# The convolution's norm, from a stage of its own into the branch stage

## What is computed

```python
y = conv(up) + conv_b                          # depthwise, 31 taps
y = jax.nn.silu(layernorm(y, ln_g, ln_b))      # mean and variance over the 1024 channels
y_c = (y * jax.nn.silu(g_conv)) @ w_conv_out   # the convolution's branch
o = sparse_attention(q, k, v, qi, ki, wi, past, rel_bias)
y_a = (o * jax.nn.silu(g_attn)) @ w_attn_out   # attention's branch
y = (gm_c * y_c + gm_a * y_a) @ w_out          # gates gm_c, gm_a per channel
```

## Time and profile before

| | us |
|---|---|
| three runs | 3887.52, 3889.7, 3890.3 (median 3889.7) |
| profiled execution, its own time | 3887.92 |
| its span | 3886.2 |
| norm stage, first issue to attention's first | 142.96 |
| branch stage, first issue to output's first | 400.00 |
| PE busy over the span | 3498.8 (90%) |
| DVE, ACT, POOL busy | 2761.4 (71%), 1359.0 (35%), 1145.0 (29%) |

### The profile page before, as it was taken

How to read it: one execution, slowest core, us unless ns; L and a number is a source line. 1 busy time by engine, 2 the same in 40 slices (tenths; PEclk the granted TensorE clock), 3 DMA queues, 4 the chain that set the end, 5 groups by cost and what they waited for, 6 DMA issues and landing times. The chain is left out here.

```text
span 3886.2 us, 50171 instructions
## 1 busy us (share of the span) xinstructions
PE 3498.8 (90%) x18975; PEld 2933.9 (75%) x18975; DVE 2761.4 (71%) x4366; ACT 1359.0 (35%) x1623; POOL 1145.0 (29%) x1004
## 2 busy tenths in 40 slices
PE   5869888999998999999753999989989998999998
PEld 1868777999998999999621555555556555999987
DVE  1431667999998699999755788787787776554434
ACT  2211556776710000100043555555545555000121
POOL 2233001543343000000003464464463332444300
PEclk9989999999999999999885999999999999999999
DMA  7274426445557344444444211211211111575643
GB/s 275 70 234 157 120 88 157 154 161 180 190 174 259 126 148 158 154 164 167 152 158 113 61 32 32 63 31 31 65 28 31 30 31 64 190 239 172 207 137 116
DMA packets 389362, 497.40 MB, mean 128 GB/s; under 512 B 52152, under 2 KB 298056, under 8 KB 388683
## 3 DMA queue, kind: packets, MB, share of 16 engines
q10 hardware_dynamic: 124144, 246.15, 18.9%
q1 hardware_dynamic: 252939, 203.55, 18.0%
q0 software_dynamic: 12112, 45.65, 3.2%
HBM read 305.62 MB, written 195.67 MB: 129 GB/s over the span
## 5 line engine op out<-in xcount | busy, mean ns | idle before, releaser
L991 PE MATMUL psum<-ha,gt 128*128 128x352 f32 x8352 | 1373.6, 325 | 46.7 <-POOL gt L629 28.6
L991 PEld LDWEIGHTS psum<-ha,gt 128*128 128x128 f32 x8352 | 1362.8, 189 | 51.2 <-POOL gt L629 28.9
L1243 DVE SCALAR_TENSOR_TENSOR cv<-cv,vecs,cv 128x1056 f32<-128x1056 f32 (+1 forms) x480 | 598.9, 1326 | 0.0
L1997 DVE TENSOR_TENSOR at_plo<-at,at 128x1024 fp32r<-128x1024 f32 (+2 forms) x308 | 402.1, 1307 | 134.8 <-ACT at L1893 133.9
L1892 ACT ACTIVATE at<-psum 128x1024 f32<-128x1024 f32 (+2 forms) x308 | 293.1, 952 | 495.2 <-PE psum L1774 495.1
L1819 PE MATMUL psum<-at,at 128*128 128x512 f32 (+5 forms) x688 | 337.9, 497 | 137.7 <-DVE at L1927 53.4
L642 PE MATMUL psum<-br,br 128*128 128x352 f32 x2304 | 375.7, 324 | 16.1 <-POOL br L620 15.5
L642 PEld LDWEIGHTS psum<-br,br 128*128 128x128 f32 x2304 | 374.0, 189 | 17.1 <-POOL br L620 13.6
L716 DVE TENSOR_SCALAR_CACHE_REDUCE gl<-gt,gl 128x1792 bf16<-128x1792 f32 (+5 forms) x325 | 383.2, 1246 | 1.2
L627 POOL TENSOR_TENSOR gt<-gt,ones 128x1024 fp32r<-128x1024 f32 x64 | 133.3, 2082 | 646.7 <-PE psum L991 522.0
L687 ACT ACTIVATE gl<-gt,gl 128x2048 bf16<-128x2048 f32 (+9 forms) x160 | 265.6, 1661 | 92.4 <-DVE gl L732 77.6
(11 more groups left out here) (239 smaller groups left out, 4783.3 us busy)
## 6 DMA issues: line engine op xcount, KB each, us to landing
scratch_ws<-gt ACTq DMA_DIRECT2D x112, 512.0 KB, 6.1
gt<-scratch_ws ACTq DMA_DIRECT2D x112, 512.0 KB, 5.0
gt<-in_w_in_dram ACTq DMA_DIRECT2D x64, 512.0 KB, 5.3
scratch_gm<-gt ACTq DMA_DIRECT2D x32, 528.0 KB, 3.1
br<-scratch_gm ACTq DMA_DIRECT2D x32, 528.0 KB, 3.6
scratch_m<-br POOLq DMA_DIRECT2D x32, 528.0 KB, 4.1
at<-scratch_q SPq DMA_DIRECT2D x128, 128.0 KB, 2.8
su<-in_ada_w_dram SPq DMA_DIRECT2D x6, 2048.0 KB, 22.3
```

Of the source, the lines that this page charges most:

```text
L991: ins = nc.tensor.matmul(of[:, j, 0:W // 3], wt[b][:, c, :], a[:, c, j * (W // 3):(j + 1) * (W // 3)], start=(c == 0 and k == 0), stop=(c ...
L1243: ins = nc.vector.scalar_tensor_tensor(to[:, 0:width], mine[:, k_:k_ + width], tap, to[:, 0:width], ALU.mult, ALU.add)
L1997: nc.vector.tensor_tensor(plo[j % 3][:, 0:len(mine), 0:n], prob[j % 3][:, 0:len(mine), 0:n], phi[j % 3][:, 0:len(mine), 0:n].bitcast(F32), ...
```

## The change

`norm_stage` and its scratch array c are gone. `branch_stage` runs (half 0, a), (half 1, a), (half 0, c), (half 1, c), all written out without loops. Beside the 8 blocks of a run with attention of half 1 (run 1) it norms the convolution's half 0, and beside run 2 half 1, in three chunks of 352 tokens each (`normed(r, slot)`: chunk q belongs to slot q of the run; each step of a chunk stands a fixed number of blocks later). y is loaded onto the place of the activations that the run before has used up (`load_y`, after that run's last product), and the normed, gated result is split in place into the high and low parts that run 2 or 3 multiplies. Sums over channels are done first by halving adds on DVE (`add_up`) or POOL (`add_squares`), and PE then needs one product for each sum (`sums`, `variance`). gc is loaded into the place of the squares (in `root`). Attention's half 0 is loaded by tiles at the start, as c's half 0 was, and its half 1 whole in block 1. The tails are turned beside run 0; their loads and stores are issued by POOL. Gated products of attention are stored to m, those of the convolution add it.

```diff
-def norm_stage(nc, mem, out, scr):
...
-        if upto >= 5:
-            norm_stage(nc, mem, out, scr)
...
-    runs = [(half, branch) for half in range(2) for branch in range(2)]
+    runs = [(half, name) for name in ("a", "c") for half in range(2)]
+    CW, NCH = W // 3, 3
+    BLOCKS = [(r, k, k % 2) for r in range(len(runs)) for k in range(KC)]
+    HALVES = 2 * KC
+        mean, var = (mem.psum[b][:, 1536:1536 + CW] for b in range(2))
+        def normed(r, slot):
+            half, j = r - 1, slot
+            return NCH * half + j if 0 <= half < 2 and 0 <= j < NCH else None
...
+            def load_y(half):
+                act.wait_ge(pr.s_mm, KC * (half + 1))
...
+            def squares(q):
+                act.wait_ge(s_diff, q + 1)
...
+            def root(q):
+                act.wait_ge(s_var, q + 1)
+                act.dma_start(square[half][:, :, at], scr["gc"]...).then_inc(s_gc[q % NCH], 16)
+                if q >= 2:
+                    act.wait_ge(s_unit, q - 1)
+                nc.scalar.activation(inv[q % 2][:], var, ACT.Ln, bias=eps[:]).then_inc(s_root, 1)
+                act.wait_ge(s_root, 2 * q + 1)
+                nc.scalar.activation(inv[q % 2][:], inv[q % 2][:], ACT.Exp, scale=-0.5).then_inc(s_root, 1)
...
+            for n, (r, k, b) in enumerate(BLOCKS):
+                load_gate(n)
...
+                if r in (1, 2) and k == 0:
+                    load_y(r - 1)
+                for q, part in ((normed(r, k - 1), squares), (normed(r, k - 3), root), (normed(r, k - 4), high), (normed(r, k - 3), swish)):
+                    if q is not None:
+                        part(q)
...
+            def add_squares(q):
+                pool.wait_ge(s_sq, q + 1)
+                for i, m in enumerate((4, 2, 1)):
+                    nc.gpsimd.tensor_tensor(sq[:, 0:m, at], sq[:, 0:m, at], sq[:, m:2 * m, at], ALU.add).then_inc(s_sqsum, 1)
...
+            for n, (r, k, b) in enumerate(BLOCKS):
+                pr.split(pool, b, n // 2)
+                if n >= 2:
+                    store(n - 2)
+                q = normed(r, k - 2)
+                if q is not None:
+                    add_squares(q)
...
+            def sums(q):
+                pe.wait_ge(s_sum, 3 * (q + 1))
...
+            def variance(q):
+                pe.wait_ge(s_sqsum, 3 * (q + 1))
+                if q:
+                    pe.wait_ge(s_unit, q)
+                nc.tensor.matmul(var, mem.mean_ones[:], square[q // NCH][:, 0, cols(q)], start=True, stop=True).then_inc(s_var, 1)
+            for n, (r, k, b) in enumerate(BLOCKS):
...
+                pr.product(pe, b, n // 2, *acts[r % 2], ready=s_flo if n == 0 else None)
+                if n in (1, 3):
+                    turn(n // 2)
+                for q, part in ((normed(r, k), sums), (normed(r, k - 2), variance)):
+                    if q is not None:
+                        part(q)
...
+            for n, (r, k, b) in enumerate(BLOCKS):
...
+                for q, part in ((normed(r, k - 1), centre), (normed(r, k), add_up), (normed(r, k - 4), gated), (normed(r, k - 3), scale),
+                                (normed(r, k - 4), low)):
+                    if q is not None:
+                        part(q)
...
+                evict(n)
```

More of the change, by code:

```diff
@@ L2030, in branch_stage @@
         s_m, s_mhi, s_mlo = sem("m"), sem("mhi"), sem("mlo")
-        sections = Sections([(r, STEPS) for r in range(len(runs))])
-        merged_before = [STEPS * (r // 2) for r in range(len(runs))]
+        s_y, s_gc = [sem(f"y{j}") for j in range(NCH)], [sem(f"gc{j}") for j in range(NCH)]
+        s_eps, s_sum, s_mean, s_diff, s_sq, s_sqsum, s_var, s_root, s_step, s_unit, s_silu, s_out, s_nhi, s_nlo = (
+            sem(n) for n in ("eps", "sum", "mean", "diff", "sq", "sqsum", "var", "root", "step", "unit", "silu", "out", "nhi", "nlo"))
@@ L2133, in step @@
[L2133 to L2141 removed]
+            tail_of = scr["u"].rearrange("(c p) t -> p c t", p=P)
+            for k, end in enumerate((SEQ, T)):
+                pool.dma_start(tails[:, :, k, :], tail_of[:, :, end - STATE:end]).then_inc(s_tail, 16)
@@ L2158, in spread @@
                 last.then_inc(s_bc, 1)
-            def step(r, i, before):
-                if not is_later(i) and r:
-                    pe.wait_ge(s_acts, 2 * KC * r)
-                for b in range(2):
-                    first = r == 0 and b == 0 and not is_later(i)
-                    pr.product(pe, b, before, *acts[r % 2], ready=s_flo if first else None)
-                if r == LAST and 1 <= i <= 2:
-                    for k in range(2):
-                        spread(2 * (i - 1) + k)
@@ L2169, in _, with turn @@
-            sections.run_unrolling_last(pe, step)
+            def turn(k):
+                pe.wait_ge(s_tail, 32)
+                if k:
+                    pe.wait_ge(s_st, 2 * k)
+                for c in range(KC):
+                    last = nc.tensor.transpose(turned[c // 4][:, (c % 4) * P:(c % 4 + 1) * P], tails[:, c, k, :], mem.ident[:])
+                last.then_inc(s_tt, 1)
+            def sums(q):
+                pe.wait_ge(s_sum, 3 * (q + 1))
+                if q:
+                    pe.wait_ge(s_diff, q)
+                else:
+                    pe.wait_ge(s_st, 4)
+                nc.tensor.matmul(mean, mem.mean_ones[:], square[q // NCH][:, 0, cols(q)], start=True, stop=True).then_inc(s_mean, 1)
```

418 lines of the change are left out of this document (164 added, 254 removed).

## The result

The changed kernel takes 3778.4 us (median of 4 runs, 3774.6 to 3783.0), the kernel before 3890.0 on the same chip: a ratio of 0.972 [0.970, 0.974], 111.6 us less. The forecast was 3813, range 3782 to 3845: the sign was right, and so were place and mechanism of two of the four long waits (chain A in both runs); the other two (chain B) did not come. The time lies 3.6 us under the range, where rival R1 stood. The profiled execution, of 3774.6 us, has a span of 3773.0 against 3886.2 before.

The account below looks back on a forecast made before the run. The norm stage was bound by hand-overs, the branch stage by PE. From 3887.9, minus 143 for the norm stage, plus 66 branch growth (6.7 + 50 + 6 + 3), gave 3811, or 3813 as median; range 3782 to 3845.

Parts of the forecast that it names:

- chain A: Steps up to the variance of chunk 1, behind block 3: PE waits 8.6 us in run 1, 11 in run 2.
- chain B: Steps from chunk 0's unit multiply to the variance of chunk 2, behind block 4: PE waits 8.3 us per normed run.
- R1: Branch stage: DVE-POOL locks hardly meet, POOL splitting while DVE waits for ACT; growth 28 to 48, 3775 to 3795; chance 0.20.
- What goes, 143: Whole norm stage before attention disappears, 143 us with 2 either way.
- Start of run 2, 6: Run 2's first sum: y issued late behind other transfers, landing about 12 us after the last block; PE waits 6.
- y's 0.5 in run 1: Run 1's first sum needs y, just inside a block's time: wait 0 to 1 us, taken as 0.5.
- late reads, 4: PE waits because DVE reads PSUM late: 1.5 us in run 1, 2.5 in run 2.
- Behind block 2 of run 2, 3: One more PE wait of 3 us there, for the mean's late turn.
- Norm's work on PE, 6.7: Branch stage: 12 small products at 0.4 us, 4.8, and 16 transposes, 1.9.
- Clock, 6: Low PE clock after five waits of 6 us or more: 6 us, or 0 if waits stay short.
- DVE and POOL: Two-SBUF-input DVE instructions and POOL elementwise work exclude each other for whole instructions; POOL's split adds 4.3 us to each chain.
- The signs: Wrong if gaps are not at L2078, all under 5 us, or PE waits for y or gc by more than 6.

Follow-up runs that it names:

- long-chain kernel: Changed kernel with ACT doing the high part of the chunk before ahead of a chunk's root; 3807.4 us, branch stage 464.9.
- kernel with the split inside B: Changed kernel with POOL's split of block 5's weights held, in runs 1 and 2, until the second chunk's Exp is done; 3783.5 us, branch stage 435.0.
- both edits: Changed kernel with ACT's root ahead of the squares and PE's variance waiting only for DVE's second small step; 3771.9 us (0.970), branch stage 429.2.
- the gate's multiply behind: DVE's scaling put ahead of the gate's multiply, against the changed kernel with root ahead of squares and three POOL holds; 3793.8 us (0.975).
- the kernel with the step's wait: Changed kernel with PE's variance waiting only for DVE's second small step, not the unit multiply; 3784.8 us (0.973), branch stage 440.3.

## Why the prediction was wrong

In terms of the profiled executions it was 3811 and came out 3774.6, 36.4 too high: 32.0 in the branch stage's growth, 4.2 in attention, which the change leaves alone, and 0.2 where attention starts. Of my 50 us of waits 19.6 came: 16.6 of the rest are chain B, 10.5 the terms at the end of run 1 and the start of run 2, 3.1 chain A.

- **What goes, 143**: right, 143.0.
- **Chain A, 8.6 and 11**: 8.1 and 8.4. Right in place, releaser and mechanism; without its 4.8 of lock it is 3.3 where I had 4.3, since gc's issue, for which I had 1.0, ran beside the squares (0.38 at 3292.68, ACTIVATE at 3292.67). In run 2 the added tile did not come on top: the sums ahead had already made PE wait 3.1 and so moved the block; that is read from the order of the rows, no run took the tile away.
- **Chain B, 8.3 twice**: 0. This is the step of the prediction that failed: its length, what PE does meanwhile, and POOL's split inside it. It is worth 16.6 directly. My 16.1 us without the lock are 13.6: silu's table load does not belong to the chain (1.28 at 3298.93, ten us ahead of the ACTIVATE that it serves), nor do the two issues on ACT's queue (3309.03 and 3310.66, beside silu, for which I had put 1.3). The earlier trace rows showed only ACTIVATEs that followed their table loads at once, so I added up what overlaps. I gave PE 12.1 us for the same stretch; it was 14.05, because the low clock behind A's wait slows block 4. And the 4.3 of lock need POOL to be at work: I put a split into both chains, while there is one for each block, released when the block two ahead of it ends: block 5's had already run in chain A, and block 6's comes at block 4's end, which meets chain B only where B is late already. The long-chain kernel and the kernel with the split inside B show that each of these, put back, brings the wait back (8.1; 2.7).
- **Start of run 2, 6, y's 0.5 in run 1, and late reads, 4**: 0 in all. They were not separate terms, but came together or not at all. Kernels whose run 1 has a wait in B of 5.9 or 8.1 have the start's too, 7.5 and 7.1, and late reads of 3.1 and 3.0. But a wait in B does not decide it: with 2.4, 2.7 and 3.3 there was neither, and with 0 (both edits) and 1.8 (the gate's multiply behind) there were 2.9 and 7.1 at the start, behind one late read of 3.9 and of 7.9. What they share is DVE, whose reads of PSUM at the end of run 1 are behind PE. The way from there to the start of run 2 can be read from ACT's queue and DVE. Kernel after:

```profile
3356.64 0.33 ACTq L1926 DMA_DIRECT2D br<-scratch_m  x1
3358.88 5.11 ACTq L1935 DMA_DIRECT2D br_y<-scratch_y  x3
...
3367.12 1.62 DVE L2121 TENSOR_TENSOR br_square<-br_y 128x1408 f32<-128x1408 f32 x1 [6.88 <-DMA br_y<-scratch_y]
```

The same rows of the kernel with the step's wait:

```profile
3365.37 0.33 ACTq L1926 DMA_DIRECT2D br<-scratch_m  x1
3365.74 9.52 ACTq L1935 DMA_DIRECT2D br_y<-scratch_y  x3
...
3379.13 3.53 DVE L2121 TENSOR_TENSOR br_square<-br_y 128x1408 f32<-128x1408 f32 x1 [13.27 <-DMA br_y<-scratch_y]
```

The gate's load for run 2 waits for DVE's read of PSUM, the old tile's (L1926) stands behind it, and y's (L1935) waits for PE's last product of run 1. In the kernel after y is issued 2.2 us behind the old tile and its first chunk lands 8.2 us later; issued 0.4 behind it, 13.4 us later. That second case is what I had priced. The other kernels lie in line: 6.4 to 8.6 us where the old tile was issued at least 2.0 ahead, 9.7 where it was 1.3 (both edits), 12.6 and 12.8 where it was 0.4. That the shared transfers make the difference is read from such rows alone; no run moved the gate's load by itself.
- **Behind block 2 of run 2, 3**: 3.1, and shown to be the lock.
- **Norm's work on PE, 6.7**: 8.1; a small product costs 0.54 and not 0.4. **Clock, 6**: 5.8, with three waits in place of five. **Rest, 3**: 1.0.
- **DVE and POOL**: right in kind. The Trainium skill, SBUF — State Buffer, section Who interferes with whom, says that a DVE instruction with two SBUF inputs and a GpSimd one block each other, and one with at most one SBUF input, outside the DVE's 2-port modes, does not. The trace agrees: the mean's subtraction, one input in PSUM, takes 3.08 beside POOL's split, where the earlier trace rows by size give 3.0; the multiply, with two, takes 5.11 beside it and 3.09 alone. The small step L2141 (a TENSOR_SCALAR) has one input, in SBUF, and yet takes 1.36 to 3.02 beside POOL in eight kernels, in place of 0.34. The section names tensor_scalar among the operations that can enter such a 2-port mode and then contend. That would fit, and so would the 0.34 against 0.53 for the step with two inputs of the same size; but no run here shows the mode.
- **R1** had the right size, for a reason that I had not given. I let POOL's split fall at the head of both chains; in A it met DVE, for 3.6 of its 4.3, in B it was absent. That the time fell where R1 stood is luck.
- **The signs** that I had set did not catch it: the gaps were at L2078, over 5, and PE did not wait for y or gc. None of the three asked whether all four gaps were there.

The Trainium skill's page ScalarE: Activation LUTs, section Table sets: the hidden batching unit, would have one load for Ln and Exp. The runs have two of 1.28 in every chain (3313.71 to 3317.37 in the kernel after, for instance), so the measurement stands.

What stays open: why the long-chain kernel's last wait in run 2 is 8.4 with A's 9.6, that is, how the waits of a run add up in general; and how much under 424.7 an order of DVE and POOL could get, since taking the norm's work out altogether gives 401.3.

## What to carry to other kernels

Before adding up the waits of several chains in one in-order engine, ask which of them can be late at the same time: a wait in the first chain delays the engine that would have waited in the second, and also the releases (of a split, of a load) that would have disturbed it. Price the chains as one timeline, and give terms that follow from another one no chance of their own. And leave out of a chain on ACT what can run ahead or beside: the table load of an ACTIVATE that waits for another engine anyway, and the DMA issues. The table loads of Ln and Exp, whose ACTIVATEs follow each other, stay in.

## What the runs showed of the hardware

- A table load runs ahead of the wait of the ACTIVATE behind it: 1.28 us at 3298.93, ACTIVATE at 3309.01. DMA issues on ACT's queue ran beside its ACTIVATEs (3309.03 to 3309.36 inside 3309.01 to 3309.69), and this one stands behind all eight of silu's ACTIVATEs in the program, which went on to 3313.69.
- The clock behind short waits of PE. Waits of 1.4 and 2.4 left the next blocks at their pace (12.09; 47.04 for four). Behind longer ones there was one exception: 2.98 left 12.07, with a granted clock of 1.00, but 2.66 gave 48.57 for four (0.60 in the first 3 us), and 2.85, 3.00 and 3.09 gave blocks of 13.61, 13.13, 12.84 and 13.14. Behind waits of 3.2 to 9.6 a block took 13.0 to 14.3, and not more behind long waits than behind short ones. The window behind the wait of 8.44, columns as above, is at half clock (1.2 GHz):

```profile
3421.20:3424.20 3.00, 2.94 (x8) 2.47 (x9) 2.34 (x2) 3.00 (x6) 0.26 (x1) 0.50 0.63 185
```

- The lock between DVE and POOL goes by whole instructions, so its price depends on where they meet: a split of 4.3 cost DVE 3.1 in four small steps, and 3.6 where it met the last of them and the multiply. On the other side, POOL's three halvings grew from 6.2 to 11.9.
